# Value pages 0 and 1 read among the last projection jobs, the later ones a pair of attention units sooner

## The reference, cut to what matters

```
def sparse_attend(q, k_sel, v_sel, valid):
    s = jnp.einsum('bqhd,bqkhd->bqhk', q, k_sel, preferred_element_type=jnp.float32) * (DSA_HEAD_DIM ** -0.5)
    s = jnp.where(valid[:, :, None, :], s, -jnp.inf)
    p = jax.nn.softmax(s, axis=-1)
    return jnp.einsum('bqhk,bqkhd->bqhd', p.astype(v_sel.dtype), v_sel)
...
def dsa_sample_attend(q, k_new, v_new, iq, iw, ik_new, cache_k, cache_v, cache_ik, page_table):
...
    v_sel = jnp.where(is_new, take_rows(v_new, n_pos), cache_v[phys, off].astype(v_new.dtype))
    return sparse_attend(q, k_sel, v_sel, valid)
```

## Time and profile before

| | |
|---|---|
| median of 3 runs | 1155.18 us (1153.79 to 1158.22) |
| the profiled execution, own time | 1159.14 us |
| its span | 1157.4 us |
| TensorE busy | 1119.2 us, 97% |
| DVE, ACT, GpSimd busy | 674.6, 494.7, 383.6 us |
| HBM read, written | 150.70 MB, 16.81 MB |

### The profile page before, as it was taken

The page is one execution under the profiler, slowest core; times in us unless marked ns, Lnnn a source line. Parts: engine busy times, 40 slices in busy tenths (PEclk is TensorE's granted clock), DMA queues, the critical chain, the costliest instruction groups (busy, mean ns, idle before and its releaser), DMA issues. The chain is left out here.

```text
span 1157.4 us, 25599 instructions
## 1 busy us (share of the span) xinstructions
PE 1119.2 (97%) x10579; PEld 977.1 (84%) x10579; DVE 674.6 (58%) x1215; ACT 494.7 (43%) x968; POOL 383.6 (33%) x321
## 2 busy tenths in 40 slices
PE   7999999899999999999999899999999999999897
PEld 6889888799758988879955389999999889888796
DVE  6462355854999689777355446596444372245742
ACT  6542376642434221222364443322453452467643
POOL 5545213243313432114300125354345245312230
PEclk9999999999999999999999899999999999999998
DMA  5235234332315787784699922233320335233212
GB/s 172 98 110 164 92 110 127 113 99 84 116 47 182 239 274 243 267 302 135 232 355 400 371 56 75 72 110 105 101 76 3 110 97 162 88 127 111 95 35 78
DMA packets 127787, 168.81 MB, mean 146 GB/s; under 512 B 20384, under 2 KB 93480, under 8 KB 127663
## 3 DMA queue, kind: packets, MB, share of 16 engines
q1 hardware_dynamic: 115609, 152.59, 39.7%
q10 hardware_dynamic: 12062, 14.59, 3.6%
HBM read 150.70 MB, written 16.81 MB: 145 GB/s over the span
## 5 line engine op out<-in xcount | busy, mean ns | idle before, releaser
L737 POOL TENSOR_TENSOR w_lo<-raw,w_hi 128x512 fp32r<-128x512 f32 (+2 forms) x267 | 361.1, 1383 | 696.0 <-ACT w_hi L1501 696.0
L773 PE MATMUL psum<-h_hi,w_hi 128*128 128x272 f32 x1616 | 471.2, 292 | 6.6 <-DVE h_lo L2425 4.7
L775 PE MATMUL psum<-h_hi,w_lo 128*128 128x272 f32 x1616 | 467.3, 289 | 0.0
L774 PE MATMUL psum<-h_lo,w_hi 128*128 128x272 f32 x1616 | 464.9, 288 | 0.0
L773 PEld LDWEIGHTS psum<-h_hi,w_hi 128*128 128x128 f32 x1616 | 303.3, 188 | 20.2 <-issue 15.3
L774 PEld LDWEIGHTS psum<-h_lo,w_hi 128*128 128x128 f32 x1616 | 303.7, 188 | 0.1
L775 PEld LDWEIGHTS psum<-h_hi,w_lo 128*128 128x128 f32 x1616 | 303.0, 187 | 0.0
L1501 ACT ACTIVATE w_hi<-raw 128x1024 fp32r<-128x1024 f32 (+1 forms) x137 | 135.5, 1034 | 117.8 <-PE psum L775 79.5
L773 PE MATMUL psum<-w_hi,h_hi 128*128 128x512 f32 (+2 forms) x352 | 124.9, 355 | 1.5 <-DVE dsa_score_s L2519 0.8
L775 PE MATMUL psum<-w_hi,h_lo 128*128 128x512 f32 (+2 forms) x352 | 121.4, 345 | 2.0 <-issue 2.0
L774 PE MATMUL psum<-w_lo,h_hi 128*128 128x512 f32 (+2 forms) x352 | 121.5, 345 | 1.3 <-issue 1.3
(11 more groups left out here) (331 smaller groups left out, 1371.8 us busy)
## 6 DMA issues: line engine op xcount, KB each, us to landing
smp_keys<-in_cache_k_dram SPq DMA_DIRECT2D x128, 256.0 KB, 4.8
raw<-in_gla_w_in_dram SPq DMA_DIRECT2D x23, 1024.0 KB, 5.3
spare<-in_cache_v_dram SPq DMA_DIRECT2D x36, 512.0 KB, 7.3
raw<-in_dsa_w_in_dram SPq DMA_DIRECT2D x17, 1024.0 KB, 5.3
raw<-in_cache_v_dram SPq DMA_DIRECT2D x28, 512.0 KB, 7.7
gla_s_in<-in_state_gla_dram SPq DMA_DIRECT2D x16, 512.0 KB, 7.8
raw<-in_gla_w_out_dram SPq DMA_DIRECT2D x8, 1024.0 KB, 6.7
out_dram<-gla_s_in ACTq DMA_DIRECT2D x16, 512.0 KB, 4.6
```

Source lines behind the costliest of these rows:

```text
L737: pool.tensor_tensor(copies(key, pair_view(w_lo, key)[:, k]), raw_copies(key, k), copies(key, pair_view(w_hi, key)[:, k].bitcast(F32)), AL ...
L773: pe.matmul(out, lh, rh, start=start, stop=False)
L774: pe.matmul(out, lh, rl, start=False, stop=False)
L775: return pe.matmul(out, ll, rh, start=False, stop=stop)
```

## The change

It has four parts. (1) The turned probabilities are written over the probabilities they came from (`pt_s[grp]` is a view of `p_s[grp]`), so each group has its own, and `ptn_s` is doubled. (2) `turn_probs` and `probs_out` work one block at a time: group 0 ahead of jobs 36, 37 and 38, group 1 in steps 5, 6 and 7, into bank 5. (3) `value_page` for page 0 stands ahead of job 41 and for page 1 ahead of job 43; page p from 2 on stands in step 2p - 3. (4) `rows_out` goes to steps 12 and 28, `turn_out` and `sample_branch` to 14 and 30, and `split_hi` of the first output weights from step 26 to step 30. The places of the value blocks and their order are the same.

```diff
+TURN_AT, EARLY_AT = (36, 37, 38), (41, 43)
+TURN_LATE = (5, 6, 7)
+PAGE_AT = tuple(range(1, 28, 2))
+ROWS_AT, OUT_TURNED = (12, 28), (14, 30)
...
-        pt_s = d("smp_pt", [P, NPAGE, P])
+        d.o += size([P, NPAGE, P], F32)
...
-        ptn_s = d("smp_ptn", [NS, P])
+        ptn_s = [d("smp_ptn", [NS, P]), at("smp_ptn1", [NS, P], F32, pt_s_at)]
...
+        pt_s = [t[:, 0:PAST].rearrange("p (g r) -> p g r", r=P) for t in p_s]
...
-                def turn_probs(grp, banks):
+                def turn_probs(grp, x, bank):
 
                     by_seq = ident[:].rearrange("p (c b x) -> p b c x", c=4, b=4)
                     pe.wait_ge(*on("p_norm", L, "sample", grp))
-                    for x in range(3):
-                        b = claim(banks[x], ("PsT", L, grp, x), ("pt_s", L, grp, x))
-                        if x < 2:
-                            for pg in range(4):
-                                o = (4 * x + pg) * PAGE
-                                mm = pe.matmul(psum[:, b, pg * P:(pg + 1) * P], p_s[grp][:, o:o + PAGE], by_seq, start=True, stop=True)
-                        else:
-                            mm = pe.matmul(psum[0:NS, b, 0:P], p_s[grp][:, PAST:KEYS], by_seq, start=True, stop=True)
-                        mm.then_inc(*sig("PsT", L, grp, x))
+                    b = claim(bank, ("PsT", L, grp, x), ("pt_s", L, grp, x))
...
+                def value_page(grp, pg):
+
+                    keys = [(L, "V", (grp * NPAGE + pg) * 2 + y) for y in range(2)]
+                    if pg == 0:
+                        pe.wait_ge(*on("pt_s", L, grp, 2))
+                        for half in range(2):
+                            claim(6 + half, ("Os", L, grp, half), (f"o_full{half}", L, grp))
+                    for key in keys:
...
-                        turn_probs(0, (6, 7, next_bank(range(2))))
+                    if f in TURN_AT:
+                        turn_probs(0, TURN_AT.index(f), (6, 7, 6)[TURN_AT.index(f)])
+                    if f in EARLY_AT:
+                        value_page(0, EARLY_AT.index(f))
                     project(f)
...
-                    if n == 2 * NPAGE - 1:
-                        turn_probs(1, (0, 1, 2))
-                    if n in (2 * NPAGE + 1, 4 * NPAGE + 1):
-                        turn_out(n // (4 * NPAGE))
+                    if n in TURN_LATE:
+                        turn_probs(1, TURN_LATE.index(n), 5)
+                    if n in OUT_TURNED:
+                        turn_out(OUT_TURNED.index(n))
                     if n < N:
                         scores(n)
-                    if (n == 0 or n % 2) and n < 4 * NPAGE - 1:
-                        value_page((n + 1) // (2 * NPAGE), (n + 1) // 2 % NPAGE)
+                    if n in PAGE_AT:
+                        value_page(*divmod(PAGE_AT.index(n) + len(EARLY_AT), NPAGE))
...
-                        probs_out(0)
+                    if f in TURN_AT:
+                        probs_out(0, TURN_AT.index(f))
...
-                    if n in (2 * NPAGE - 1, 4 * NPAGE - 1):
-                        rows_out(n // (4 * NPAGE - 1))
-                    if n == 2 * NPAGE - 1:
-                        probs_out(1)
-                    if n == 4 * NPAGE + 2:
+                    if n in ROWS_AT:
+                        rows_out(ROWS_AT.index(n))
+                    if n in TURN_LATE:
+                        probs_out(1, TURN_LATE.index(n))
+                    if n == OUT_TURNED[1] + 1:
...
-                    if n == 2 + last_spare[0][2] // 2 * 2:
+                    if n == len(units) - 2:
...
-                    if n in (2 * NPAGE - 1, 4 * NPAGE - 1):
-                        rows_out(n // (4 * NPAGE - 1))
-                    if n in (2 * NPAGE + 1, 4 * NPAGE + 1):
-                        sample_branch(n // (4 * NPAGE))
+                    if n in ROWS_AT:
+                        rows_out(ROWS_AT.index(n))
+                    if n in OUT_TURNED:
+                        sample_branch(OUT_TURNED.index(n))
```

More of the change, by code:

```diff
@@ new lines, in value_page @@
+                def value_page(grp, pg):
[5 more added lines that the diff above has]
+                    for key in keys:
+                        pe.wait_ge(*on(f"raw{slot[key]}", key))
+                    for half in range(2):
+                        for bl in range(4):
+                            r = slice(bl * NS, (bl + 1) * NS)
+                            o = (bl % 2) * D + half * BLK
+                            mm = pe.matmul(psum[r, 6 + half, :], pt_s[grp][:, pg, r], held(slot[keys[bl // 2]])[:, o:o + BLK],
+                                           start=pg == 0, stop=False)
+                    mm.then_inc(*sig("pages_used", keys[0], also=((keys[1],),)))
+                    if pg == NPAGE - 1:
+                        for half in range(2):
+                            for bl in range(4):
+                                r = slice(bl * NS, (bl + 1) * NS)
+                                mm = pe.matmul(psum[r, 6 + half, :], ptn_s[grp][:, r],
+                                               v_d[0:NS, SMP, half * BLK:(half + 1) * BLK], start=False, stop=True)
+                        mm.then_inc(*sig("Os", L, grp))
@@ L1395, in values_of @@
                     mm.then_inc(*sig("O", L, n))
[L1397 to L1419, removed]
                 def turn_out(grp):
@@ L1917, in sample_exp, with probs_out @@
                                    accum_out=ast[:, 3 + grp, 2:3]).then_inc(*sig("p_exp", L, "sample", grp))
-                def probs_out(grp):
-                    for x in range(3):
-                        act.wait_ge(*on("PsT", L, grp, x))
-                        b = bank_of("PsT", L, grp, x)
-                        if x < 2:
-                            copy(pt_s[:, 4 * x:4 * x + 4, :], psum[:, b, :].rearrange("p (g r) -> p g r", g=4))\
-                                .then_inc(*sig("pt_s", L, grp, x))
-                        else:
-                            copy(ptn_s[:], psum[0:NS, b, 0:P]).then_inc(*sig("pt_s", L, grp, x))
+                def probs_out(grp, x):
+                    act.wait_ge(*on("PsT", L, grp, x))
+                    b = bank_of("PsT", L, grp, x)
+                    if x < 2:
+                        copy(pt_s[grp][:, 4 * x:4 * x + 4, :], psum[:, b, :].rearrange("p (g r) -> p g r", g=4))\
+                            .then_inc(*sig("pt_s", L, grp, x))
+                    else:
+                        copy(ptn_s[grp][:], psum[0:NS, b, 0:P]).then_inc(*sig("pt_s", L, grp, x))
                 last_early = max(p for p in range(2 * NPAGE) if PAIR_AREA[p] == 0)
```

7 lines of the change are left out of this document (added).

## The result

| | before | changed |
|---|---|---|
| median | 1155.82 us (1153.79 to 1158.22, 4 runs) | 1171.05 us (1169.85 to 1174.28, 4 runs) |
| profiled execution, own time | 1159.14 us | 1171.96 us |
| its span | 1157.4 us | 1170.2 us |

The changed kernel is slower: ratio 1.0127, 95% interval 1.0104 to 1.0150, some 15 us. The forecast was 1164.4 us in a range up to 1171.2. The direction and the mechanism of the early waits were right. The size was not: the result lies 0.15 us inside the upper end of the range, which is luck, and the loss is 15 us where 9.2 were forecast.

A forecast was written before the change was run, and what follows sets the result against it. The prediction took TensorE's idle time and clock in 560 to 680 us as the bound. Its terms summed to +9.2 us on the profiled 1159.14 us, 1168.3, less 4.0 to the median: 1164.4 us, range 1151.4 to 1171.2.

The forecast's parts named there:

- The bound: TensorE has 97% of the span; with matmuls unchanged, its idle time and clock in 560 to 680 us decide.
- Part 1: Probabilities turned in jobs 36 to 38 and units 5 to 7: the wait before unit 15 goes, -0.5 us.
- Part 2: Pages 0 and 1 ahead of job 43's end: no wait themselves, but the value stream starts 3.7 us later.
- Page 2: In unit 1, TensorE waits for a value block that has not landed: +4.3 us (3.5 to 5.6).
- Page 3: In unit 3, a second, smaller wait for a value block: +1.2 us (0.3 to 2.0).
- The end of the stream: From page 13's release to page 15: idle 5.5 us against 4.8, +0.7 us (-1.3 to +1.8).
- `split_hi`: In unit 30 on ACT, its copies stand ahead of unit 29's `att_pt` copy: +1.0 us (nothing to 2.0).
- The clock: Falls after idle time: early, behind the new waits, +2.5 us (0 to 5.8); late as now, 0 (-5.8 without the fall).
- The sum: All terms together, +9.2 us on the profiled execution; 1168.3 us, taken to 1164.4 us as the median.
- Rival 1: Idle time comes as forecast but the clock stays up, early and late: +0.9 us, 1156.1 us; chance 0.22.
- Rival 2: Blocks freed sooner bring page 15's blocks in time, late idle and clock loss vanish: -7.3 us, 1147.9 us; chance 0.12.
- Rival 3: Job 43's end does not bind, so the value stream starts where it did: some +4 us, 1159 us; chance 0.08.

The follow-up runs named there:

- e2: The changed kernel with value pages, `rows_out`, `turn_out` and `split_hi` in their old steps, only the early turning kept: 1156.88 us, ratio 1.0000 to before.
- e3: The changed kernel with V5 to V8 in the places that pages 0 and 1 free, V9 and V10 in the last gate weights' memory: 1167.52 us, ratio 1.0081.
- e6: The kernel before with one more wait on SyncE, so V5 is issued only when page 1 has been read: 1167.04 us, ratio 1.0091.
- e7: The kernel of e4 with the first output weights loaded behind V31 and `split_hi` in step 27: 1157.21 us, ratio 1.0001 to before.
- e11: The kernel before with the first output weights loaded behind V31 and `split_hi` in step 29: 1150.84 us, ratio 0.9946.
- e1: The changed kernel with `split_hi` of the first output weights back in step 26: 1167.11 us, ratio 1.0073 to before.
- e5: The kernel before with only `split_hi` of the first output weights moved from step 26 to step 30: 1161.51 us, ratio 1.0041.
- e4: The changed kernel with both edits, other places for V5 to V10 and `split_hi` in step 26: 1162.66 us, ratio 1.0040 to before.
- e8: The kernel of e7 with pages 2 to 15, `rows_out` and `turn_out` in their old steps, `split_hi` in step 29: 1154.92 us, ratio 0.9982 to before.
- e9: The kernel of e8 with pages 2 to 7 in steps 1 to 11 and pages 8 to 15 in steps 15 to 29: 1152.87 us, ratio 0.9959 to before.

## Why the prediction was right, and where it was short

- **The bound** (TensorE's idle time and clock in 560 to 680): right in the main. Of the 12.8 us between the two profiled executions 9.6 lie between the end of job 43 and the first output product, the two pages moved ahead of it counted in. Job 43 ends 1.0 us later than the pages alone make it (584.17 against 579.47 + 3.7), and behind the first output product (677.4 before, 688.0 now) 480.0 us are left before and 482.2 now, 0.7 of that by the clock up to 690 and 1.7 by a fall in 935 to 939 that the trace of before does not have.
- **Part 1, the turning, -0.5:** e2 measured 0 with an interval of 0.15% on either side, too wide to tell the two apart. The wait named did go; a wait for a gate copy (0.58 us, bank order) came, which the term had not.
- **Part 2, the restart of the stream 3.7 us later:** right. V5 went out at 584.63 instead of the 583.8 forecast, 4.5 us later than before, of which the two pages are 3.7; e3 took the cause away, e6 put it alone into the kernel before.
- **Page 2, +4.3:** 3.48 us, after the 0.58 for the gate copy; together 4.1. **Page 3, +1.2:** 1.01.
- **The end of the stream, +0.7:** 5.0 us of wait for page 15 against the 5.5 forecast, 4.8 before, so +0.2. Right; and e7 and e11 show that what stands between page 13's release and these blocks decides it, in the queue or on the DMA engines.
- **`split_hi`, +1.0 (0 to 2.0): this is the term that failed.** Its size was bounded by the length of the two copies, 2.0 us, as if they could delay TensorE once. In fact they stand ahead of both the exponential of unit 31 and the copy of unit 29: TensorE waited 1.82 us for `att_pt` and then 2.16 for `att_p`, and the clock was at 0.50 from 683 to 689, in the last unit. e1 and e5 measure the whole, with its clock, at 0.54 and 0.41% of the time, about 6 and 5 us.
- **The bare end, no term:** 1.27 us of wait for `att_p` at 671.36, and smaller ones, come with page 15 two steps sooner and the softmax chain of the last long units without a page over it. e4, with `split_hi` back in its place, still has the 1.27. The prediction put this at nothing, without a reason.
- **The clock, early +2.5, late 0:** the fall behind page 2 cost 1.7 us, inside the 0 to 5.8 given. Late I took before's loss (5.8 as I counted it) as unchanged, and it is 4.6 now, at two places: behind page 15 (1.7) and in the last units (2.9), where the second is `split_hi`'s. Such a fall is not the same each time: around page 15 the clock was down for 3.5 us in this execution, for 14 in that of e1 and for 18 in that of e3. I also misread: the idle 0.96 and 1.06 us of those two stretches are one wait across their border,

```profile
509.06 0.28 PE L775 MATMUL psum<-w_hi,h_lo 128*128 128x256 f32 x1 [2.02 <-issue]
```

so the row I took for a fall behind two pieces of 1 us shows one behind a single piece of 2.02. The Trainium skill describes such falls for a kernel that waits for DMA between bursts of matmuls (page "TensorE: Matmul & The Clock Gate", section "HAM oscillation — how this bites in real kernels"); the trace agrees for the two waits for value blocks, of 3.48 and 5.01 us, each with a fall right behind it. The third fall came behind waits for ACT and DVE.
- **The sum:** +9.2 was forecast against the profiled execution, and +12.8 came. The median of before was then reached by taking 4.0 us off, as if the changed kernel's executions lay around its own trace as before's did. They don't: its trace is 0.9 us above its median, before's 3.3 above (of four runs). Of the 6.7 us between the forecast and the result that is 3.1, and the terms are 3.6; together they all but took the result out of the range.
- **Rival 1** (the clock stays up) did not happen. **Rival 2** (the blocks freed sooner bring the stream's end in time) did not happen either; page 15's blocks in time came only with another order of the loads, which the change did not have (e11, a gain of 0.54%). **Rival 3** (job 43's end does not bind) is refuted by the restart at 584.63 and by e3.

## What to carry to other kernels

When a step is moved ahead of an instruction, look at who waits for that instruction's end, and at the whole in-order queue behind that waiter: two page reads of 3.7 us ahead of job 43 held back 27 blocks. In a stream through few buffers, the last loads are decided by the release they wait for and by what is queued between, so a large load that is needed later belongs behind them. And a copy in a queue that feeds a three-engine chain is to be put where the chain is waiting anyway; its cost elsewhere is not its length, but each link that it delays, and then the clock.

## What the hardware showed that I had not expected

- In 490 to 700 us of the thirteen traces TensorE has 18 idle pieces of 2.02 us or more (2.02 and 2.17 before; 3.48, 5.01 and 2.16 changed; 2.49 in e8), and with each the clock fell to 0.50, its lower level of 1.2 GHz, in the piece or within three us behind it. No piece of 1.0 to 1.78 us brought it down by itself, though several stood within ten microseconds (e9: 0.88 and 1.46, with 1.00 behind both). Of nine between 1.82 and 1.94 that began at full clock six did and three did not (e3's 1.88 did, e1's 1.94 did not), where two of the six had a second wait of 2.2 us 1.2 us behind them, in which the clock fell. A wait of 1.5 to 2.4 us between 508 and 516 us is in each version, which may be part of the scatter between executions.
- Idle time is not all that goes ahead of a fall. In the changed kernel the clock was down in 935 to 939 (0.57) with no idle piece of more than 0.53 us in the 15 us ahead of it, and the traces of e2, e3, e5 and e9 have a fall of four to five us at this place of the program, the other eight have none.
- The value stream ran at 409 GB/s over 20 us from HBM, in both kernels. The Trainium skill gives about 358 GB/s as the limit on the HBM side for such loads (page "DMA: Bandwidth & Descriptors", section "Where 436 GB/s comes from"), and reports single-core transfers of up to 425 GB/s just above it, with the other core of the pair idle; this core was alone, and the measurement goes with the second figure.
- A change of how often one job draws from a rotating pair of banks moved a 0.58 us wait to the first attention unit, in every version that had the early turning (the cause, the order of the banks, is read from the program).

Not tried: the early turning together with e11, the order of the loads changed without the place of `split_hi`, and an order in which the gate's copy and `scores(0)` use different banks. Why waits of about 1.9 us bring the clock down in one kernel and not in another is not settled by these runs.
